# The sample group of an RWKV-7 projection as one step of 160 columns, with its features kept on chip

## The chip, the cores and the metric

The kernel runs as one program on 1 core of a Trainium2 chip. The metric is the device time of one execution in microseconds (us). Of the kernel before there are three timed executions and one that the hardware profiler recorded. PE is TensorE, DVE VectorE, ACT ScalarE, POOL GpSimd and SP SyncE, which here only issues transfers.

## The reference

One step of a decoder trunk for two groups of tokens: a prompt of 2048 tokens, and a sample group of 8 sequences with 4 new tokens each. Both pass through an RMSNorm, a combined projection, RWKV-7 time mixing (8 heads of 64), dilated attention (8 heads of 64), an output projection and a mixture of experts. All is float32. The part that matters here is what the projection hands to the time mixing:

```python
r = r_c + mu[0] * (r_p - r_c)          # c: this token, p: the token before
k = k_c + mu[1] * (k_p - k_c)
v = v_c + mu[2] * (v_p - v_c)
w_log = -softplus(-(w0 + tanh(xw @ w1) @ w2)) - 0.5
decay = exp(-exp(w_log))
a = sigmoid(a0 + (xa @ a1) @ a2)
g = sigmoid(xg @ g1) @ g2
kk = heads(k * k_k)
kk = kk * rsqrt(max(sum(kk * kk, -1), 1e-24))
k_h = heads(k) * (1.0 + (a_h - 1.0) * k_a)
# per token: s = s * w + (s @ -kk) (kk * a) + v k;  y = s @ r
bonus = sum(r_h * k_h * r_k, -1) * v_h
```

## The kernel before

The program is a chain of stages (`projection`, `rwkv_chunks`, `attention`, `output_projection`, the experts). Each stage is a block of five instruction streams, one per engine, written out by hand in the order in which they run and tied by semaphores. The block's end (L54) is a barrier: no engine starts the next stage before all have finished, and SP reaches it only after the stores of the stage have landed.

**The projection.** It takes the 2048 prompt tokens in `NP` = 8 chunks of 256 columns, channels on the partitions. A chunk has four channel groups m = 0..3 of 128 channels. For each group PE multiplies out k, r, v (`channels`), the rates a and the gate g (`rates`), the cumulated log decay (`cumulate`), and two sums over the heads (`norm_sums` for the norm of kk, `bonus_sums`). ACT scales with the token-shift weights (`scale`), applies sigmoid (`rates`), square, exp (`exponents`) and sqrt (`norm_roots`); sigmoid, exp and sqrt each need a table of their own, so each group loads three (`ACT_TABLE_LOAD`). DVE makes five feature rows per token (`mix_k`, `mix_r`, `mix_v`, `bonus_terms`, `recurrence_rows`) and the gate rows (`gate_rows`).

The sample group follows as chunk `n == NP`. It has only `WS` = 40 columns: 8 sequences of 4 tokens with the shifted-in token ahead of each. Its projections are made the other way round, tokens on the partitions: `sample_pair(i)` multiplies two of the six 512-column blocks (k and r, v and query, key and value) with 40 columns as weights, 32 matmuls of 512 columns each. DVE copies the result out (`pair_copy`), and `sample_channels` turns one channel group of k, r or v at a time back to channels on partitions. Then the four groups run through the same code as a prompt chunk, one after the other, 40 columns at a time. `cumulate(NP, m)` waits for `rk_read` of group m - 1, so the groups form one chain. `sample_pair(2)` stands in the middle of group 1.

The recurrence wants the features of two sequences as a tile of 64 token slots each, of which the sample fills 4. POOL therefore clears such rows (`UF` and the projection's weights `W`, four memsets), the groups write into them, and SP stores each group to `ft_s` in device memory (`store_units`): four transfers of 320 KB and one of decays, 4 KB in pieces of 8 bytes. A gate store of 32 KB follows (`store_gates`). ACT may not write the gate of group m before the gate store of group m - 2 has landed (`g_st`). The last stores end the stage.

**The recurrence.** `rwkv_chunks` takes 16 prompt tiles and then 4 sample tiles, n = 16..19, of two sequences each. PE's order is written as iterations: iteration i runs the inverse of tile i, the head (`turn`, products) of tile i + 1 and the tail of tile i - 1. Features sit in a ring of four tiles `F[n % 4]`, each 128 x 2568. SP loads tile n + 4 once the state of tile n is done (`s_ready[1]`). POOL copies identity blocks into `T` for each tile once the tail of tile n - 3 has read them (`hg_done`), and issues three or four stores of zero rows between. The tile's state `s_ready` is DVE's `state`.

## Time and profile before

| | |
|---|---|
| median of 3 executions (lowest, highest) | 3448.79 us (3446.48, 3475.65) |
| the profiled execution, its own time | 3453.1 us |
| its span, mean granted PE clock | 3451.3 us, 0.951 |
| PE, DVE, ACT, POOL busy | 91%, 38%, 29%, 10% |
| projection, from its last prompt matmuls | sample part from 906.2 us |
| recurrence | begins at 982.1 us |

The span is the profiled execution from its first to its last instruction; its own time is 1.8 us more. A PE that is busy 91% of the span still leaves stretches in which it hardly works. The stretch from 906.2 to 982.1 us is one of them: it is the sample group's part of the projection and the wait for its stores. In the rows below, times are counted from the start of the span, "idle before" is what the engine waited and for whom, and a matmul on float32 is recorded as two instructions, a transpose as one.

### The profile page before, as it was taken

How to read it: one execution, taken by the hardware profiler on the slowest of the kernel's cores; microseconds unless marked ns; L12 is line 12 of the kernel's file. 1: busy time of each engine (PE TensorE's matmuls, PEld its weight loads, DVE VectorE, ACT ScalarE, POOL GpSimd, SP SyncE). 2: the span in 40 equal slices, each digit the busy share in tenths (PEclk: the TensorE clock that was granted, in tenths of full speed). 3: DMA queues.
4: the chain of work that ended last, by engine and by line, in shares of the span. 5: the costliest groups of instructions: out<-in, count | busy, mean ns of one | idle time of the engine just before them, and what ended most of it. 6: DMA issues, size and time to landing. Idle time of an engine off the chain costs nothing. (4 is left out here: it accounts for less than half of the span.)

```text
span 3451.3 us, 74888 instructions
## 1 busy us (share of the span) xinstructions
PE 3146.2 (91%) x30921; PEld 2149.7 (62%) x30922; DVE 1318.3 (38%) x3229; ACT 1013.0 (29%) x2151; POOL 338.4 (10%) x351
## 2 busy tenths in 40 slices
PE   6999999999859988988999979996999999999990
PEld 4667666676458888877767765554555555555550
DVE  3455344553224443435655436664111111111117
ACT  3334433344122222225544433331111111111112
POOL 0000000000110000003333000001101001010104
PEclk9999999999979999999999859997999999999995
DMA  6111111111273333326666446423768786677658
GB/s 209 63 71 65 51 46 63 70 55 45 72 180 113 120 137 120 119 98 204 183 182 179 125 162 193 154 80 123 278 242 284 239 283 223 227 277 245 233 193 306
DMA packets 299029, 544.42 MB, mean 158 GB/s; under 512 B 98146, under 2 KB 122466, under 8 KB 292116
## 3 DMA queue, kind: packets, MB, share of 16 engines
q1 hardware_dynamic: 252860, 401.29, 34.6%
q10 hardware_dynamic: 25128, 66.26, 6.1%
q0 software_dynamic: 20784, 73.15, 5.8%
q8 instruction: 197, 3.23, 0.4%
q14 instruction: 60, 0.49, 0.0%
HBM read 400.66 MB, written 139.98 MB: 157 GB/s over the span
## 5 line engine op out<-in xcount | busy, mean ns | idle before, releaser
L307 PE MATMUL proj_main_ps<-proj_xt,proj_w 128*128 128x257 f32 x1536 | 351.1, 381 | 0.0
L307 PEld LDWEIGHTS proj_main_ps<-proj_xt,proj_w 128*128 128x128 f32 x1536 | 290.2, 191 | 41.1
L2544 PE MATMUL moe_y_ps<-moe_w,moe_ht 128*64 128x512 f32 x1312 | 301.2, 601 | 3.1 <-ACT moe_ht L2583 3.1
L2292 PE MATMUL out_proj_ps<-out_w,out_ct 128*128 128x512 f32 x544 | 241.6, 598 | 6.1 <-DMA out_w<-in_w_out_dram 6.1
L337 PE MATMUL proj_main_ps<-proj_w,proj_xt 128*128 128x512 f32 x512 | 225.3, 593 | 0.0
L2594 ACT ACTIVATE moe_sg<-moe_gate 128x256 f32<-128x256 f32 x82 | 31.4, 383 | 535.7 <-PE moe_gate L2528 535.7
L2544 PEld LDWEIGHTS moe_y_ps<-moe_w,moe_ht 128*64 128x64 f32 x1312 | 87.3, 137 | 158.6 <-issue 155.3
L2292 PEld LDWEIGHTS out_proj_ps<-out_w,out_ct 128*128 128x128 f32 x544 | 101.7, 192 | 121.8 <-issue 120.5
L2630 DVE COPY moe_y<-moe_y_ps 128x512 f32<-128x512 f32 x82 | 56.7, 691 | 313.8 <-PE moe_y_ps L2544 313.8
L1190 DVE COPY_PREDICATED rwkv_t<-ahead_rwkv_cons,rwkv_level_ps 128x512 f32<-128x512 uint32 (+1 forms) x168 | 109.1, 660 | 175.7 <-PE rwkv_level_ps L908 175.4
L337 PEld LDWEIGHTS proj_main_ps<-proj_w,proj_xt 128*128 128x128 f32 x512 | 97.2, 190 | 108.4 <-issue 107.0
L1667 DVE CUSTOM_DVE_ANT_0 att_sc<-att_s_ps,ahead_mask 128x256 f32<-128x256 f32 (+1 forms) x384 | 117.2, 361 | 118.4 <-PE att_s_ps L1474 118.4
L908 PE MATMUL rwkv_level_ps<-rwkv_t,rwkv_w 64*64 64x64 f32 x2688 | 153.2, 221 | 2.7 <-issue 2.7
L2528 PE MATMUL moe_up<-moe_w,moe_xt 128*64 128x256 f32 x1344 | 154.3, 382 | 0.0
L2528 PE MATMUL moe_gate<-moe_w,moe_xt 128*64 128x256 f32 x1344 | 152.2, 379 | 0.0
L2579 ACT COPY moe_xt<-moe_xt_ps 128x512 f32<-128x512 f32 x83 | 48.6, 585 | 343.4 <-PE moe_xt_ps L2521 343.4
L2528 PE MATMUL moe_gate<-kept_first_gate,moe_xt 128*64 128x256 f32 x1280 | 147.5, 384 | 1.4 <-ACT moe_xt L2579 1.4
L2528 PE MATMUL moe_up<-kept_first_up,moe_xt 128*64 128x256 f32 x1280 | 146.9, 382 | 0.0
L1576 ACT ACTIVATE att_sc<-att_sc,att_nm 128x256 f32<-128x256 f32 (+1 forms) x384 | 145.6, 451 | 3.9 <-issue 3.1
L1509 PE MATMUL att_o_ps<-att_v,att_pt 128*128 128x65 f32 x768 | 142.0, 301 | 0.0
L2636 DVE TENSOR_TENSOR moe_hd<-moe_sg,moe_gate 128x256 f32<-128x256 f32 x82 | 34.6, 421 | 280.0 <-ACT moe_sg L2594 280.0
L1474 PE MATMUL att_s_ps<-att_kt,ahead_qt 64*128 64x256 f32 (+1 forms) x768 | 139.8, 493 | 0.9 <-DVE att_pt L1675 0.5
(362 smaller groups left out, 5535.3 us busy)
## 6 DMA issues: line engine op xcount, KB each, us to landing
moe_w<-in_expert_w_dram SPq DMA_DIRECT2D x64, 2048.0 KB, 9.6
y_rows<-rwkv_zero POOLq DMA_DIRECT2D x65, 512.0 KB, 4.8
kept_first_gate<-in_expert_w_dram SPq DMA_DIRECT2D x16, 2048.0 KB, 9.6
kept_first_up<-in_expert_w_dram SPq DMA_DIRECT2D x16, 2048.0 KB, 14.9
y_rows<-moe_y ACTq DMA_DIRECT2D x164, 128.0 KB, 6.0
ft_p<-proj_uf SPq DMA_DIRECT2D x32, 642.0 KB, 3.2
rwkv_feat<-ft_p SPq DMA_DIRECT2D x12, 1284.0 KB, 6.9
att_s_k<-in_cache_att_k_dram ACTq DMA_DIRECT2D x14, 1024.0 KB, 6.8
```

The source lines that it names most:

```text
L307: last = mm(out[:, 0:w + 1], W[:, k, kind * C + m * P:kind * C + (m + 1) * P], XT[n % 2][:, k, 0:w + 1], start=(k == 0), stop=(k == KT - 1))
L337: last = mm(out[:], XT[n % 2][:, k, 1 + i // 2 * P:1 + (i // 2 + 1) * P], W[:, k, j * C:(j + 1) * C], start=(k == 0), stop=(k == KT - 1))
L908: last = mm(level_ps[g][part(c), hh * P + DH:(hh + 1) * P], W[g][part(c), hh, :], T[i % 3][part(c), h, DH:P], start=True, stop=True, skip_ ...
L1190: v.copy_predicated(T[i % 3][:, 4 * g:4 * g + 4, k0:P], wide(level(l)[:, k0:P], 4).bitcast(U32), four(level_ps[g][:])[:, :, k0:P]).then_in ...
L1474: last = mm(s_ps[u % 2][e][:, pl * 2 * P + k_from(u):(pl + 1) * 2 * P], QT[rows, q, q_at:q_at + d * (P - 1) + 1:d], KT[rows, q, k_at:k_at ...
L1509: last = mm(out, PT[u % 2][:, hl, 1, :], V[n % NV][:, h, :], start=first(u), stop=True, skip_group_check=True)
L1576: nc.scalar.activation(SC[u % NSC][:, hl, k0:], SC[u % NSC][:, hl, k0:], ACT.Exp, bias=NM[:, n, 4 * half + hl:4 * half + hl + 1], scale=-1 ...
L1667: v.tensor_tensor_reduce(SC[u % NSC][:, hl, k0:], s_ps[u % 2][e][:, pl * 2 * P + k0:(pl + 1) * 2 * P], mask[:, k0:], 1.0, 3e38, ALU.add, A ...
L2292: last = mm(proj_ps[j][:], CT[t % 2][:, k, :], W[:, k, 512 * j:512 * (j + 1)], start=(k == 0), stop=(k == KT - 1))
L2528: last = mm(bank[j * HB:(j + 1) * HB, 0:HF], XT[:, q, r * HB:(r + 1) * HB], W[:, k, j * HF:(j + 1) * HF], start=(k == 0), stop=(k == KT - ...
L2544: last = mm(py[j * HB:(j + 1) * HB, :], HT[:, c, r * HB:(r + 1) * HB], W2[s][:, k, j * 512:(j + 1) * 512], start=(k == 0), stop=(k == FE / ...
L2630: v.tensor_copy(Y[:], py[:]).then_inc(y_ev, 1)
```

## The change

The four channel groups of the sample are no longer run one after the other. PE makes the rates of all four in a row, then pair 1, the four cumulations, the twelve transposes of k, r and v, pair 2, and then one norm sum and one bonus sum over 160 columns, in separate parts of one bank. ACT and DVE treat 160 columns at once where the operand has no constant per channel group, and in four pieces of 40 where it has one. Sigmoid, exp and sqrt are each used once. `NR` is gone: the norms are now made in `KK`, in the prompt's chunks too.

The features go to `sample_feat`, 128 x 5 x 128 on chip, and the decays to `sample_decay`, 128 x 32. They outlive the stage. `ft_s` and its stores are gone, and so are POOL's four memsets in the projection. The gate is stored once, 128 KB. In the recurrence, POOL builds each sample tile (`spread`): one memset of 128 x 2568, two copies of 80 elements per partition and one of 8. PE waits for it (`f_spread`) where it waited for the load.

```diff
                 s = slot(n, m)
                 sp.wait_ge(units, step(n, m) + 1)
                 sp.wait_ge(pc_copied, step(n, m) + 1)
-                if n < NP:
-                    sp.dma_start(ft_p[TT * n:TT * n + TT, :, m, :].rearrange("t p k -> p t k"), UF[:, s]).then_inc(u_st[s], 16)
-                else:
-                    rows = sample_rows_of(m).rearrange("p j (t c) k -> p t j (c k)", c=2)
-                    for t in range(SB // 2):
-                        sp.dma_start(ft_s[t, :, m, 0:5 * P].rearrange("p (j k) -> p j k", j=5), rows[:, t]).then_inc(u_st[s], 16)
-                    sp.dma_start(ft_s[:, :, m, 5 * P:FT].rearrange("t p c -> p t c"), sample_decay_of(m).rearrange("p (t c) -> p t c", c=2)).then_inc(u_st[s], 16)
+                sp.dma_start(ft_p[TT * n:TT * n + TT, :, m, :].rearrange("t p k -> p t k"), UF[:, s]).then_inc(u_st[s], 16)
...
+            sp.dma_start(next_F[0], ft_p[0]).then_inc(feat_ld[0], 16)
+            sp.dma_start(next_consts, next_consts_in).then_inc(cons_ld, 16)
+            sp.dma_start(shift_s_out, XN[SJ - 1:TS:SJ, :]).then_inc(shift_st, 16)
+            for i in range(3):
+                store_kv(NP, i)
+            sp.wait_ge(bonus, 4 * NP + 1)
...
-            g.wait_ge(bonus, 4 * NP)
-            for j in range(2):
-                g.wait_ge(u_st[j], 32 * NP)
-            nc.gpsimd.memset(UF[:], 0.0).then_inc(padded, 1)
-            g.wait_ge(filled, pair_job(1) + 1)
-            for m in range(1, 4):
-                nc.gpsimd.memset(W[:, 0:5, (m - 1) * SB * CH:m * SB * CH], 0.0).then_inc(padded, 1)
...
-            def sample_channels(kind, m):
-                i, part = (0, upper) if kind == 1 else (0, lower) if kind == 0 else (1, upper)
-                out = begin_job(job(NP, (1, 0, 2).index(kind), m))
-                pe.wait_ge(emptied, pair_job(i) + 1)
-                nc.tensor.transpose(out[:, 1:WS + 1], PAIRS[i][part, m * P:(m + 1) * P], ident[part, part]).then_inc(filled, 1)
...
+            def sample_turn_kr():
+                pe.wait_ge(emptied, pair_job(0) + 1)
+                for m in range(4):
+                    sample_turn(0, upper, x_ps, m * WS, m)
+                    last = sample_turn(0, lower, lz_ps[1], m * WS, m)
+                last.then_inc(s_turned, 1)
+
+            def sample_turn_v():
+                pe.wait_ge(emptied, pair_job(1) + 1)
+                pe.wait_ge(ag_read, 4 * NP + 1)
+                for m in range(4):
+                    last = sample_turn(1, upper, ag_ps, m * WS, m)
+                last.then_inc(s_v_turned, 1)
+
...
+            def sample_cumulate():
+                pe.wait_ge(z_ready, NP + 1)
+                pe.wait_ge(rk_read, 4 * NP)
+                for m in range(4):
+                    last = mm(own(c_ps, m), Z[0:WS, 0, m * P:(m + 1) * P], cum_s[0:WS, :], start=True, stop=True, skip_group_check=True)
+                last.then_inc(cum_done, 1)
+
+            def sample_norm_sums():
+                pe.wait_ge(sq_ready, 4 * NP + 1)
+                pe.wait_ge(exps, 4 * NP + 1)
+                mm(c_ps[:, SW:2 * SW], same_head, SQ[:, 0:SW], start=True, stop=True, skip_group_check=True).then_inc(kk_done, 1)
+
+            def sample_bonus_sums():
+                pe.wait_ge(rk_ready, 4 * NP + 1)
+                pe.wait_ge(root, 4 * NP + 1)
+                mm(c_ps[:, 2 * SW:3 * SW], same_head, RK[:, 0:SW], start=True, stop=True, skip_group_check=True).then_inc(rk_done, 1)
 
...
             sample_pair(1)
-            for m in range(4):
-                sample_channels(1, m)
-                if m >= 1:
-                    rates(NP, m)
-                    bonus_sums(NP, m - 1)
-                sample_channels(0, m)
-                cumulate(NP, m)
-                sample_channels(2, m)
-                norm_sums(NP, m)
-                if m == 1:
-                    sample_pair(2)
-            bonus_sums(NP, 3)
+            sample_cumulate()
+            sample_turn_kr()
+            sample_turn_v()
+            sample_pair(2)
+            sample_norm_sums()
+            sample_bonus_sums()
 
...
             def norm_roots(n, m):
                 u = step(n, m)
                 a.wait_ge(kk_done, u + 1)
                 if u >= 1:
-                    a.wait_ge(unit, u)
-                nc.scalar.sqrt(NR[:, 0:width(n)], c_ps[:, 0:width(n)]).then_inc(root, 1)
+                    a.wait_ge(units, u)
+                nc.scalar.sqrt(KK[:, 0:width(n)], c_ps[:, 0:width(n)]).then_inc(root, 1)
+
+            def sample_rate_acts():
+                a.wait_ge(s_rated, 1)
+                a.wait_ge(units, 4 * NP)
+                for m in range(4):
+                    last = act(own(A, m), own(ag_ps, m), ACT.Sigmoid, bias=col(A0, m))
...
+            def sample_exponents():
+                a.wait_ge(cum_done, 4 * NP + 1)
+                a.wait_ge(units, 4 * NP)
+                act(EXS[:, 1:SW + 1], c_ps[:, 0:SW], ACT.Exp, scale=-DECAY)
+                act(EX2[:, 0:SW], c_ps[:, 0:SW], ACT.Exp, scale=DECAY).then_inc(exps, 1)
+                a.wait_ge(exps, 4 * NP + 1)
+                nc.scalar.copy(sample_decay, EXS[:, 1:SW + 1].rearrange("p (b j) -> p b j", j=SQ1)[:, :, SQ1 - 1]).then_inc(pc_copied, 1)
+
+            def sample_roots():
+                a.wait_ge(kk_done, 4 * NP + 1)
+                a.wait_ge(units, 4 * NP)
+                nc.scalar.sqrt(KK[:, 0:SW], c_ps[:, SW:2 * SW]).then_inc(root, 1)
 
             square(0)
...
+            sample_rate_acts()
+            sample_exponents()
+            sample_scale_kr()
+            sample_squares()
+            sample_scale_v()
+            sample_roots()
             for i in range(1, 3):
...
+            def sample_recurrence_rows():
+                u = 4 * NP
+                tok = lambda x: tokens(x[:, 0:SW])
+                v.wait_ge(exps, u + 1)
+                v.tensor_tensor(sample_unit(1), tok(R), tok(EXS[:, 1:]), ALU.mult)
+                v.tensor_tensor(sample_unit(3), tok(KH), tok(EX2), ALU.mult)
+                v.wait_ge(root, u + 1)
+                v.tensor_scalar(KK[:, 0:SW], KK[:, 0:SW], 1e-12, None, ALU.max).then_inc(bound, 1)
+                v.wait_ge(bound, u + 1)
+                v.reciprocal(KK[:, 0:SW], KK[:, 0:SW]).then_inc(inverse, 1)
+                v.wait_ge(inverse, u + 1)
+                for m in range(4):
+                    last = stt(own(KK, m), own(K, m), col(K_K, m), own(KK, m), ALU.mult, ALU.mult)
+                last.then_inc(unit, 1)
+                v.wait_ge(unit, u + 1)
+                stt(sample_unit(0), tok(KK), -1.0, tok(EXS), ALU.mult, ALU.mult).then_inc(a_done, 1)
+                v.wait_ge(a_done, u + 1)
+                v.tensor_tensor(KK[:, 0:SW], KK[:, 0:SW], A[:, 0:SW], ALU.mult).then_inc(kka, 1)
+                v.wait_ge(kka, u + 1)
+                v.tensor_tensor(sample_unit(2), tok(KK), tok(EX2), ALU.mult).then_inc(units, 1)
+
+            def sample_gate_rows():
+                v.wait_ge(rk_done, 4 * NP + 1)
+                v.wait_ge(s_v_mixed, 1)
+                v.tensor_tensor(tokens(RK[:, 0:SW]), sample_unit(4), tokens(c_ps[:, 2 * SW:3 * SW]), ALU.mult).then_inc(rk_read, 1)
+                v.wait_ge(rk_read, 4 * NP + 1)
+                for m in range(4):
+                    last = stt(by_seq(sample_gates[:, m, 1, :]), tokens(own(RK, m)), col(LN_B, m), tokens(own(GG[0], m)), ALU.add, ALU.mult)
+                last.then_inc(bonus, 1)
 
...
         def _(sp):
             def load(n):
-                sp.dma_start(F[n % 4][:], ft_p[n] if n < NP else ft_s[n - NP]).then_inc(f_ld[n % 4], 16)
+                sp.dma_start(F[n % 4][:], ft_p[n]).then_inc(f_ld[n % 4], 16)
...
-                if n + 4 < NT:
+                if n + 4 < NP:
...
+            def spread(n):
+                g.wait_ge(s_ready[1], n - 3)
+                nc.gpsimd.memset(F[n % 4][:], 0.0).then_inc(f_cleared, 1)
+                g.wait_ge(f_cleared, n - NP + 1)
+                rows = F[n % 4][:, :, 0:5 * P].rearrange("p m (j c k) -> p m j c k", j=5, c=2)
+                for c in range(2):
+                    nc.gpsimd.tensor_copy(rows[:, :, :, c, 0:given_feat.shape[4]], given_feat[:, :, :, 2 * (n - NP) + c, :])
+                nc.gpsimd.tensor_copy(F[n % 4][:, :, 5 * P:FT], given_decay[:, :, 2 * (n - NP):2 * (n - NP) + 2]).then_inc(f_spread, 1)
+
...
+                if n >= NP:
+                    spread(n)
                 if n >= 3:
...
                 if half == 0:
-                    pe.wait_ge(f_ld[n % 4], 16 * (n // 4 + 1))
+                    if n < NP:
+                        pe.wait_ge(f_ld[n % 4], 16 * (n // 4 + 1))
+                    else:
+                        pe.wait_ge(f_spread, n - NP + 1)
```

PE, projection, after the low-rank products of the sample. L320 is `sample_pair`, L347 the decay's projection, L354 and L355 the rates, L314 the transposes, L365 `cumulate`, L371 and L376 the two head sums. Before:

```order
L320 MATMUL proj_main_ps<-proj_w,proj_xt 40x512 x16
L314 MATMUL proj_main_ps<-proj_consts,proj_x 128x40 x2
L365 MATMUL proj_c_ps<-proj_consts,proj_z 128x40
L314 MATMUL proj_main_ps<-proj_consts,proj_x 128x40
L371 MATMUL proj_c_ps<-proj_sq,proj_consts 128x40
L314 MATMUL proj_main_ps<-proj_consts,proj_x 128x40
L354 MATMUL proj_ag_ps<-proj_lta,proj_a 128x40
L355 MATMUL proj_ag_ps<-proj_ltg,proj_g 128x40
L376 MATMUL proj_c_ps<-proj_rk,proj_consts 128x40
L314 MATMUL proj_main_ps<-proj_consts,proj_x 128x40
...
L371 MATMUL proj_c_ps<-proj_sq,proj_consts 128x40
L320 MATMUL proj_main_ps<-proj_w,proj_xt 40x512 x16
```

Now (L335 `sample_pair`, L310 and L311 the rates, L318 cumulations, L291 the transposes, L324 and L329 the head sums):

```order
L362 MATMUL proj_lz_ps<-proj_w2x,proj_ltw 40x512
L310 MATMUL proj_ag_ps<-proj_lta,proj_a 128x40
L311 MATMUL proj_ag_ps<-proj_ltg,proj_g 128x40
...
L335 MATMUL proj_main_ps<-proj_w,proj_xt 40x512 x16
L318 MATMUL proj_c_ps<-proj_consts,proj_z 128x40 x4
L291 MATMUL proj_x_ps<-proj_consts,proj_x 128x40
L291 MATMUL proj_lz_ps<-proj_consts,proj_x 128x40
...
L291 MATMUL proj_ag_ps<-proj_consts,proj_x 128x40 x4
L335 MATMUL proj_main_ps<-proj_w,proj_xt 40x512 x16
L324 MATMUL proj_c_ps<-proj_sq,proj_consts 128x160
L329 MATMUL proj_c_ps<-proj_rk,proj_consts 128x160
```

The third pair moved from the middle of group 1 to a place behind every transpose and ahead of both head sums, and the head sums of four groups became one each.

ACT, projection, one group of the sample (group 1) before; L497 to L504 are the rates, L481 `scale`, L511 the squares, L521 to L530 the exponents, L537 the roots:

```order
L497 ACT_TABLE_LOAD
L497 ACTIVATE proj_a<-proj_ag_ps,proj_par 128x40
...
L504 ACTIVATE proj_kh<-proj_a,proj_less,proj_par 128x40
L481 ACTIVATE proj_ev<-proj_main_ps,proj_par 128x40
L511 ACTIVATE proj_sq<-proj_k,proj_par 128x40
L521 ACT_TABLE_LOAD
L521 ACTIVATE proj_exs<-proj_c_ps 128x40
L522 ACTIVATE proj_ex<-proj_c_ps 128x40
L530 COPY proj_w<-proj_exs 128x8
L481 ACTIVATE proj_ev<-proj_main_ps,proj_par 128x40
L537 ACT_TABLE_LOAD
L537 ACTIVATE proj_nr<-proj_c_ps 128x40
```

Now, from the rates of all groups to the end of the stage's arithmetic:

```order
L542 ACTIVATE proj_a<-proj_ag_ps,proj_par 128x40 x4
L547 COPY proj_gg<-proj_ag_ps 128x160
L549 ACTIVATE proj_gb<-proj_ag_ps,proj_par 128x32 x4
L553 ACTIVATE proj_kh<-proj_a,proj_less,proj_par 128x40 x4
L581 ACT_TABLE_LOAD
L581 ACTIVATE proj_ex<-proj_c_ps 128x160
L582 ACTIVATE proj_ex<-proj_c_ps 128x160
L561 ACTIVATE proj_ev<-proj_x_ps,proj_par 128x40 x4
...
L575 ACTIVATE proj_sq<-proj_k,proj_par 128x40 x4
L589 ACT_TABLE_LOAD
L589 ACTIVATE proj_kk<-proj_c_ps 128x160
```

Three table loads per group became two for all groups, since the first sigmoid finds its table loaded. The exponents moved ahead of the scaling of k and r.

SP, the end of the projection, before (L188 the sample's query, key and value rows, L166 and L167 `store_units`, L175 the gate; one group of four is shown) and now:

```order
L188 DMA qkv_s<-proj_x 8x512 x8
L166 DMA ft_s<-proj_w 128x5x128 x4
L167 DMA ft_s<-proj_w 128x4x2
L175 DMA gt_s<-proj_gb 128x2x32
L166 DMA ft_s<-proj_w 128x5x128 x4
L167 DMA ft_s<-proj_w 128x4x2
L175 DMA gt_s<-proj_gb 128x2x32
L54 UNCONDITIONAL_BRANCH
```

```order
L224 DMA ahead_feat<-ft_p 128x2568
L225 DMA ahead_rwkv_cons<-in_const_rwkv_chunks_dram 128x1280
L226 DMA out_dram<-proj_xn 8x1024
L180 DMA qkv_s<-proj_x 8x512 x12
L230 DMA gt_s<-proj_gb 128x256
L54 UNCONDITIONAL_BRANCH
```

Twenty transfers to `ft_s` and three gate stores are gone, and nothing stands behind the one gate store that is left.

## Rows read from the trace of the kernel before

**Rows 1.** Windows of the stage's end: engines busy (instructions), clock granted, DMA share, GB/s

```profile
945.10:967.20 22.10, 6.08 (x28) 4.96 (x27) 8.59 (x41) 12.63 (x30) 0.00 (x0) 0.61 0.98 126
967.20:982.10 14.90, 0.00 (x0) 0.00 (x0) 0.00 (x0) 0.00 (x0) 0.00 (x0) 0.50 0.91 102
```

**Rows 2.** Timeline where the two orders part: start us, us, engine, line, operation

```profile
915.28 0.41 PE L354 MATMUL proj_ag_ps<-proj_lta,proj_a 64*128 64x40 f32 x2
...
915.96 7.07 PE L320 MATMUL proj_main_ps<-proj_w,proj_xt 128*40 128x512 f32 x32
...
922.96 0.26 PE L314 MATMUL proj_main_ps<-proj_consts,proj_x 40*128 40x40 f32 x2
...
923.04 0.39 PE L365 MATMUL proj_c_ps<-proj_consts,proj_z 40*128 40x40 f32 x2
```

**Rows 3.** Groups of instructions, 906.2 to 967.2 us: count, busy, mean ns, idle before

```profile
L521 ACT ACT_TABLE_LOAD x4 | 5.1, 1283 | 0.1
L537 ACT ACT_TABLE_LOAD x4 | 5.1, 1283 | 0.1
L497 ACT ACT_TABLE_LOAD x3 | 3.8, 1283 | 6.2 <-DVE proj_w L662 3.4 <-DVE proj_uf L662 2.8
```

**Rows 4.** Timeline, sample group 0 and the start of group 1

```profile
923.10 6.58 POOL L270 MEMSET proj_w<- 128x2560 f32 x3 [51.05 <-PE proj_main_ps L320]
...
926.46 0.62 PE L371 MATMUL proj_c_ps<-proj_sq,proj_consts 128*128 128x40 f32 x2 [2.32 <-ACT proj_ex L522]
...
928.30 1.42 DVE L651 TENSOR_SCALAR proj_nr<-proj_nr 128x40 f32<-128x40 f32 x1 [1.17 <-ACT proj_nr L537]
...
931.22 1.28 ACT L497 ACT_TABLE_LOAD   x1 [2.77 <-DVE proj_uf L662]
...
932.51 0.29 ACT L497 ACTIVATE proj_a<-proj_ag_ps,proj_par 128x40 f32<-128x40 f32 x1
```

**Rows 5.** Timeline, pair 2 in the middle of group 1

```profile
936.09 8.93 PE L320 MATMUL proj_main_ps<-proj_w,proj_xt 128*40 128x512 f32 x32
```

**Rows 6.** Timeline, the same chain at 40 columns (group 2) and at 256 (prompt)

```profile
861.97 0.38 ACT L537 ACTIVATE proj_nr<-proj_c_ps 128x256 f32<-128x256 f32 x1
...
866.15 0.43 DVE L662 TENSOR_TENSOR proj_uf<-proj_kk,proj_ex 128x256 f32<-128x256 f32 x1
...
866.72 0.60 DVE L611 SCALAR_TENSOR_TENSOR proj_mixed<-proj_diff,proj_mu,proj_xt 128x40 f32<-128x40 f32 x3
...
953.37 0.20 ACT L537 ACTIVATE proj_nr<-proj_c_ps 128x40 f32<-128x40 f32 x1
...
955.01 0.19 DVE L662 TENSOR_TENSOR proj_w<-proj_kk,proj_ex 128x32 f32<-128x32 f32 x1
```

**Rows 7.** Timeline, end of the stage and start of the next

```profile
952.46 5.15 SPq L188 DMA_DIRECT2D qkv_s<-proj_x  x8
...
966.89 0.25 DVE L671 SCALAR_TENSOR_TENSOR proj_gb<-proj_rk,proj_par,proj_gg 128x32 f32<-128x32 f32 x1
...
972.88 1.55 SPq L175 DMA_DIRECT2D gt_s<-proj_gb  x1
...
982.10 1.29 SPq L823 DMA_DIRECT2D rwkv_feat<-ft_p  x3
```

**Rows 8.** Waits of SP's queue, 900 to 1500 us: total, times, longest

```profile
SPq L245 <- DMA gt_s<-proj_gb: 7.0, 1, 7.0
```

**Rows 9.** Transfers, whole span: KB each, median us from issue to landing

```profile
qt_p<-proj_q SPq DMA_DIRECT2D x32, 128.0 KB, 1.7
```

**Rows 10.** Timeline of the recurrence: sample tile 19 fetched, and shortly before its turn

```profile
1497.43 0.32 SPq L823 DMA_DIRECT2D rwkv_feat<-ft_s  x1
...
1500.85 0.91 DVE L1190 COPY_PREDICATED rwkv_t<-ahead_rwkv_cons,rwkv_level_ps 128x256 f32<-128x256 uint32 x2 [3.44 <-PE rwkv_level_ps L908]
...
1520.61 1.11 PE L1027 MATMUL rwkv_head_ps<-ahead_rwkv_cons,rwkv_nat 128*128 128x128 f32 x4 [3.15 <-DMA rwkv_nat<-in_state_rwkv_dram]
```

**Rows 11.** Timeline, POOL's clearing of 2568 elements in the projection

```profile
869.82 2.24 POOL L267 MEMSET proj_uf<- 128x2568 f32 x1 [173.35 <-DMA ft_p<-proj_uf]
```

More of the change, by code:

```diff
@@ L209, in _ @@
             load_next(3)
-            for n in range(NP + 1):
+            for n in range(NP):
                 for m in range(4):
@@ new lines, in sample_squares @@
+            def sample_squares():
+                a.wait_ge(s_mixed, 1)
+                a.wait_ge(kk_done, 4 * NP)
+                for m in range(4):
+                    last = act(own(SQ, m), own(K, m), ACT.Square, scale=col(K_K, m))
+                last.then_inc(sq_ready, 1)
+            def sample_exponents():
[5 more added lines that the diff above has]
+                nc.scalar.copy(sample_decay, EXS[:, 1:SW + 1].rearrange("p (b j) -> p b j", j=SQ1)[:, :, SQ1 - 1]).then_inc(pc_copied, 1)
```

250 lines of the change are left out of this document (141 added, 109 removed).

## The prediction

> **What bounds the kernel now.** I read the windows of the projection's end first, then the order of instructions there, then the waits, and last the recurrence. Over the whole run PE is busy 91%, so only stretches where PE does little can be shortened. From 945.1 to 967.2 us PE is busy 6.08 of 22.1 us, ACT 12.63 and DVE 8.59: no engine is full, so a chain of waits sets the pace. From 967.2 to 982.1 us no engine does anything while the DMA engines are 0.91 busy [rows 1]: these are the stores. What is to be seen is that the sample's part of the stage consists of a chain at 40 columns, where fixed costs count and widths do not, and of a tail of transfers.
>
> Within a group, each table load takes 1.28 us and falls on the chain, because it is started only after the wait for the product that needs it [rows 3, 4]. There are 4 for exp, 4 for sqrt and 3 for sigmoid from 923 us on. PE's clock is granted at a mean of 0.61 of full speed from 945.1 us and at 0.50 from 967.2 (0.50 is 1.2 GHz, 1.00 is 2.4 GHz), and pair 2 takes 8.93 us where pair 1 takes 7.07 [rows 1, 2, 5].
>
> **The change, part by part.** Both orders agree up to 915.28 us, where the rates begin [rows 2]. I lay the new chain from there.
>
> 1. Rates of four groups: the two matmuls of one group take 915.28 to 915.96, 0.68 us. Four take 2.72, to 918.00. Before, one group stood ahead of pair 1.
> 2. Pair 1, by the starts 915.96 and 922.96: 7.00 us, to 925.00 [rows 2].
> 3. Four cumulations of 0.39 us each at most: 1.56, to 926.56. Twelve transposes, two in 0.26 us: 1.56, to 928.12 [rows 2]. The transposes of v wait for DVE's copy of pair 1, 512 columns wide and begun at 925.1, and for ACT's rate work, which has 7 us during pair 1 for 13 instructions; both are done by about 926.
> 4. Pair 2 directly behind: 7.00, to 935.12. That takes the full clock. PE has no gap over a few tenths between 915 and 935 now, while the clock fell before only after the gap of 2.32 us ahead of 926.46 [rows 4].
> 5. Behind pair 2, ACT and DVE must not be late. After 926.56: table 1.28, two exponentials of 0.38 (the width of 256 is an upper bound), a copy 0.20, eight scalings of 0.29, eight DVE mixes of 0.20 (three take 0.60), four squares of 0.29 [rows 4, 6]. Without any overlap that is 926.56 + 1.28 + 0.96 + 2.32 + 1.60 + 1.16 = 933.9 us. So the norm sum starts when pair 2 ends, and all this costs nothing; without pair 2 as cover it would be up to 5.8 us.
> 6. Norm sum over 160 columns: 0.60 us, the 0.62 of the narrow one at low clock being near [rows 4]. To 935.7.
> 7. Table for sqrt, 1.28 us, to 937.0.
> 8. From the start of sqrt to the last feature row: 953.37 to 955.20, 1.83 us, at 40 columns, and 861.97 to 866.58, 4.61 us, at 256 [rows 6]. In a straight line, 160 columns give 1.83 + 2.78 x 120/216 = 3.37. The product with k_k is now four pieces, three more starts of 0.18 us from three in 0.60: +0.53. To 940.9.
> 9. Gate rows: one product of about 0.3 and four pieces, 0.78. To 942.0, against 967.14 before [rows 7]. The chain gains **25.1 us**.
>
> The tail: before, the last arithmetic ends at 967.14 and the next stage starts at 982.10, 14.96 us. The last gate store is issued at 972.88, held up by five stores ahead of it, and SP waits 7.0 us more for it [rows 7, 8]. Now the same wait has one store of 128 KB, 1 KB per partition, behind it nothing. The query stores are of just that size and shape and land in a median of 1.7 us [rows 9]. With 0.8 us to see the last result, issue and pass the barrier, 2.5 us. This end could also be as slow as now: 7.0 + 1.55 + 0.6 = 9.2 us [rows 7, 8]. I take 2.5, because the 7.0 stands behind 1.3 MB of feature stores in pieces of 512 and of 8 bytes that no longer exist. The 16 small stores of queries, keys and values that are left by then are issued by SP and ACT side by side, 8 each. SP took 5.15 us for eight of them before [rows 7], so from 935.8 on to 941, before the gate. The tail gains **12.4 us**.
>
> The rest of the edits. Sqrt into `KK` in the prompt's chunks waits for `units` instead of `unit`; ACT has already waited for `units` of the same step ahead of the exponents, so nothing. The carry copies on POOL have no memset behind them, nothing. In the recurrence POOL adds per tile a memset of 2.24 us [rows 11] and three copies of at most 80 elements, 1.2 us together if each is 0.4. The tile's predecessor is free at 1497.4 us, when SP now issues the load, and PE turns tile 19 only after 1520.61 [rows 10]. 3.5 us fit into 23 us; the identity copy of the same tile has the time of one iteration too. Cost nothing, and if that cover were gone, 3.5 us for each of four tiles.
>
> Sum: 25.1 + 12.4 = **37.5 us**, from 3453.1 of the profiled execution to 3415.6. Its own time lies 4.3 us above the median of the three, so against that median **3411.3 us**, 1.1% less.
>
> A table load has no wait behind it in the trace: it starts at 931.22, takes 1.28 and sigmoid starts at 932.51 [rows 4]. The Trainium skill (ScalarE: Activation LUTs, What ACT_TABLE_LOAD costs) puts a drain of 1.38 us beside the load of 1.283, 2.66 us in all. By it, step 7 would be 1.4 us longer and the result 3412.7 us; the load's own figure agrees with the trace, the drain does not.
>
> **The rivals.**
>
> A. The gate store lands late. It starts while 16 small stores are in flight, 8 rows of 2 KB each from few partitions. For it: every gate store of the sample waited long before. Against it: those had the feature stores ahead. At the 9.2 us above: 30.8 us gained, 3418 us. Chance 0.15.
>
> B. The clock falls before pair 2. The transposes and cumulations are 40 columns wide and small work. Then pair 2 takes 8.93 instead of 7.00, and cumulations and transposes twice as long in part, +1.5, and the head sum a little more: 34 us gained, 3415 us. Against it: pair 1 ran at full speed behind narrow matmuls too. Chance 0.12.
>
> C. POOL's memset holds up DVE. One memset of POOL ran from 923.10 to 929.68, and DVE's maximum on `proj_nr`, one input and output on chip, took 1.42 us from 928.30 and ended at 929.72, with it; products with two inputs went on beside it [rows 4]. In the recurrence a memset of 2.24 us starts when a state is done. DVE's next work there comes 3.44 us after its last [rows 10], so 1.2 us at most would stick out behind memset and copies, and no DVE instruction there is of the kind that was held. If each were held for the full 2.24 us: 9 us back, 3420 us. Chance 0.08.
>
> The Trainium skill (SBUF — State Buffer, Who interferes with whom) has it as a lock on a port pair that the two share: whoever comes second waits for the whole instruction, if DVE uses both ports or has two inputs on chip while POOL reads. That rule speaks against moving clearing work beside DVE; the row of 1.42 us agrees with it.
>
> D. Slower than before. `spread` becomes what PE waits for. PE waits in order at `turn`, so everything behind stands. It decides only above the cover of 23 us a tile; to be 1% slower than before, four tiles would have to lose 37.5 + 34.5 = 72 us, 18 each, so one `spread` would have to last 41 us. That would happen if the strided copies of 80 elements took some 19 us each, and would give about 3483 us. Nothing in the trace is near: POOL clears 2568 elements in 2.24 us [rows 11]. Chance 0.03.
>
> **How the numbers follow.** The forecast has 0.62, A 0.15, B 0.12, C 0.08, D 0.03. The predicted time is that of the forecast. The range goes down to 3404, where steps 3, 6 and 8 are over by 3 us and executions scatter by 3 or 4 us, and up to 3425, above the cases A to C and two of them partly together; outside are D, the larger combinations and a disturbed set of executions. What a measurement can tell here from no change is about 1%, 34.5 us, and 3414.3 us is the bound. The forecast lies 3 us beyond it, so I give it 0.78 to pass; B 0.4, A and C 0.15: 0.48 + 0.05 + 0.04 = 0.57 faster. Slower 0.03, the rest 0.40 the same.
>
> **What would show it.** In the profile of the changed kernel: the next stage starts near 944.5 us; pair 2 takes 7.1 us and the norm sum stands right behind it (if it is idle before, step 5 is wrong); two table loads behind the rates; the last gate row near 942; one gate store landing in about 2 us (9 means A); no wait of PE for POOL in the recurrence, whose length from its start stays within 2 us (C or D otherwise). The prediction would be wrong if the recurrence or a later stage became longer by what the projection gives.

## The result, and the profile after

The changed kernel takes 3396.05 us (median of 4 executions, 3392.17 to 3402.42), the kernel before 3457.14 in the same comparison (4 executions): ratio 0.984, 95% interval 0.980 to 0.989. Two more comparisons gave 0.988 (0.984 to 0.993) and 0.986 (0.982 to 0.990), over 1% faster in each. The forecast was 3411.3 us with a range from 3404: the direction is right, the time fell below the range. Three later executions of 5036 to 8071 us, far slower than all others, are left out of every figure below.

The profiled execution has a span of 3399.8 us against 3451.3, so 51.5 us are to be placed. I take the same marks in both traces: the copy of pair 0 by DVE, the first copy of `rwkv_t` (recurrence), the copy of `rwkv_sv` (its end), the first product of `out_ct` (attention's end).

| us | before | changed | gained |
|---|---|---|---|
| up to pair 0's copy | 914.5 | 913.8 | 0.8 |
| from there to the recurrence | 67.6 | 28.2 | 39.4 |
| recurrence | 592.3 | 593.2 | -0.9 |
| attention | 482.4 | 470.5 | 11.9 |
| all that follows | 1394.5 | 1394.1 | 0.4 |

The projection gives 39.4 us, where the prediction had 37.5. Another 11.9 come from attention, whose code the change doesn't touch.

First the windows of the changed sample part, which answer to [rows 1]:

```profile
core 0: us, PE busy (x) PEld busy (x) DVE busy (x) ACT busy (x) POOL busy (x), PEclk, DMA share, GB/s
914.50:925.80 11.30, 11.30 (x71) 5.75 (x70) 0.69 (x1) 5.28 (x17) 0.00 (x0) 1.00 0.01 1
925.80:932.80 7.00, 7.00 (x34) 1.89 (x33) 3.25 (x17) 4.81 (x19) 0.00 (x0) 1.00 0.03 11
932.80:938.10 5.30, 1.02 (x6) 0.57 (x4) 5.00 (x17) 0.30 (x1) 0.00 (x0) 0.75 0.08 28
938.10:942.00 3.90, 0.00 (x0) 0.00 (x0) 0.02 (x1) 0.00 (x0) 0.00 (x1) 0.50 0.19 63
```

PE is busy without a gap, at the full clock, until pair 2 is done; only 5.3 us are left in which DVE alone is the chain, and the tail is 3.9 us instead of 15. Now the order of instructions of the changed kernel in time, the chain's links only:

```profile
914.52 0.41 PE L310 MATMUL proj_ag_ps<-proj_lta,proj_a 64*128 64x40 f32 x2
...
917.27 7.07 PE L335 MATMUL proj_main_ps<-proj_w,proj_xt 128*40 128x512 f32 x32
...
920.38 1.28 ACT L581 ACT_TABLE_LOAD   x1
924.26 0.86 PE L318 MATMUL proj_c_ps<-proj_consts,proj_z 40*128 40x40 f32 x6
...
925.38 0.31 ACT L581 ACTIVATE proj_ex<-proj_c_ps 128x160 f32<-128x160 f32 x1 [3.72 <-PE proj_c_ps L318]
...
925.78 7.07 PE L335 MATMUL proj_main_ps<-proj_w,proj_xt 128*40 128x512 f32 x32
...
930.03 0.82 ACT L568 ACTIVATE proj_ev<-proj_ag_ps,proj_par 128x40 f32<-128x40 f32 x4
930.87 1.28 ACT L589 ACT_TABLE_LOAD   x1
...
932.77 0.54 PE L324 MATMUL proj_c_ps<-proj_sq,proj_consts 128*128 128x160 f32 x2
...
933.35 0.30 ACT L589 ACTIVATE proj_kk<-proj_c_ps 128x160 f32<-128x160 f32 x1 [1.20 <-PE proj_c_ps L324]
...
933.62 6.52 ACTq L635 DMA_DIRECT2D out_dram<-proj_x  x8
...
933.90 0.23 DVE L776 TENSOR_SCALAR proj_kk<-proj_kk 128x160 f32<-128x160 f32 x1
934.17 1.15 DVE L778 RECIPROCAL proj_kk<-proj_kk 128x160 f32<-128x160 f32 x1
...
937.38 0.74 DVE L796 SCALAR_TENSOR_TENSOR proj_gb<-proj_rk,proj_par,proj_gg 128x32 f32<-128x32 f32 x4
939.06 0.68 SPq L230 DMA_DIRECT2D gt_s<-proj_gb  x1
941.99 1.28 SPq L935 DMA_DIRECT2D rwkv_feat<-ft_p  x3
```

Both table loads stand ahead of the instruction that needs them, and in ScalarE's idle time: each ends before PE's product does. The chain's last row ends at 938.12 (967.14 before), the recurrence starts at 941.99 (982.10 before, [rows 7]).

Last, the recurrence's new work, POOL's instructions in order of time for tile 16 (answers to the memset of [rows 11]):

```profile
1382.70 2.24 POOL L983 MEMSET ahead_feat<- 128x2568 f32 x1 [20.47 <-DVE rwkv_s L1344]
1385.00 0.45 POOL L987 COPY ahead_feat<-ahead_sample_feat 128x80 f32<-128x80 f32 x2
1385.39 0.20 POOL L988 COPY ahead_feat<-ahead_sample_decay 128x8 f32<-128x8 f32 x1
1388.97 1.04 POOL L997 COPY rwkv_t<-ahead_rwkv_cons 128x1024 f32<-128x1024 f32 x1 [3.39 <-PE rwkv_tail_ps L1096]
```

A spread lasts 2.9 us, and POOL then idles 3.39 us for PE. No row has PE waiting for POOL.

### The profile page after: what moved, and what is told of

Read it like the earlier page. It is cut to its first block and busy times, and to the rows that moved or that the text cites. A ratio compares the mean times of both kernels' runs of the same rounds, so it can differ in the third digit from the quotient of the medians.

```text
span 3399.8 us, 74730 instructions
## 1 busy us (share of the span) xinstructions
PE 3123.1 (92%) x30909; PEld 2127.4 (63%) x30910; DVE 1311.9 (39%) x3202; ACT 999.8 (29%) x2127; POOL 342.5 (10%) x362
## 5 line engine op out<-in xcount | busy, mean ns | idle before, releaser
L1031 PEld LDWEIGHTS rwkv_level_ps<-rwkv_t,rwkv_w 64*64 64x64 f32 x2688 | 134.9, 137 | 8.1 <-issue 8.1
```

Of the source, the lines that this page charges most:

```text
L1031: last = mm(level_ps[g][part(c), hh * P + DH:(hh + 1) * P], W[g][part(c), hh, :], T[i % 3][part(c), h, DH:P], start=True, stop=True, skip_ ...
```

## The experiments

Theory 1: the change is worth what the projection's chain and tail give, and the 12 us of attention are chance. Theory 2: the change also shortens attention. Beside these, single terms of the sum are measured.

**before_again** and **after_again**: the two kernels unchanged.

> The kernel before, once more. The change took 51.5 us off the profiled span, 40.1 of it by the start of the recurrence and 12 in the attention stage (last state copy of the recurrence to the first head product of the output projection: 482.3 us before, 470.5 changed), which the change does not touch. Theory 1 (chance): TensorE's clock falls to 0.50 for some tens of us while TensorE is fully busy in attention, in a place and for a length that differs from execution to execution; then attention here is anywhere between 465 and 485 us, and the ratio of this kernel to itself is 1.000 within about 0.005. Theory 2 (caused): attention is again within 3 us of 482.

> The changed kernel, once more. Theory 1: the attention stage may well be 475 us or more in this profile, and over many executions the change is worth what the projection gives, 39 to 40 us (ratio 0.9885). Theory 2: attention is within 3 us of 470.5 again and the ratio is about 0.985, 51 to 54 us. Both expect the recurrence to start at 942 us.

Measured: the kernel before 3440.33 us (12 executions) against its own 3439.89 (29 more), ratio 1.000 (0.997 to 1.004); the changed kernel 3398.26 (6), ratio 0.988 (0.984 to 0.993). In their profiled executions the sample part takes 66.1 and 28.2 us, attention 466.0 and 462.7. So the gain of attention is 3.3 us here and was 11.9: it isn't a property of the change alone. The windows show what is. Kernel before, then the same stretch (391 us into attention) of before_again:

```profile
1954.50:1961.60 7.10, 7.10 (x17) 2.36 (x15) 0.00 (x0) 0.00 (x0) 0.00 (x0) 1.00 0.21 52
1961.60:1965.00 3.40, 3.40 (x25) 3.02 (x26) 2.92 (x11) 0.74 (x3) 0.00 (x0) 0.84 0.02 5
1965.00:2010.00 45.00, 45.00 (x239) 41.01 (x238) 16.29 (x108) 22.68 (x72) 0.00 (x0) 0.50 0.27 73
```

```profile
1963.60:2008.60 45.00, 45.00 (x329) 37.86 (x327) 21.97 (x146) 29.22 (x91) 0.00 (x0) 1.00 0.35 91
```

PE is busy all 45 us in both, but at 0.50 it gets through 239 matmuls and at 1.00 through 329 (a rough comparison, since the second stretch begins some 7 us earlier in the program, with 3.6 us of the long products named below in it). It fell behind 7.1 us in which PE had only the sample's products of values, with every other engine at 0.00:

```profile
1954.53 6.17 PE L1529 MATMUL att_t_ps<-att_s_v,att_s_lm 128*96 128x512 f32 x14
1960.63 1.09 PE L1530 MATMUL att_t_ps<-att_s_vn,att_s_pn 4*96 4x512 f32 x2
```

The same products stand there in every execution, and in 11 of 14 profiled ones the clock stays at this place. In the changed kernel's trace it fell earlier, 189 and 237 us into attention, also directly behind such products (at 1721.4 and 1770.5 us), and for some 10 us each. Over the 14 profiled executions of all kernels here I added up the time at half clock in windows of 1 us in which PE was busy 90% or more: attention took 459 to 463 us where it was 4 to 16 us, 466 to 475 where it was 27 to 51, and 480 to 482 where it was 74 to 79.

**compact_groups**: the features on chip and `spread`, but still four groups one after the other.

```diff
-                    for t in range(SB // 2):
-                        sp.dma_start(ft_s[t, :, m, 0:5 * P]..., rows[:, t]).then_inc(u_st[s], 16)
+        unit_of = ... sample_feat[:, j, m * TS:(m + 1) * TS].rearrange("p (b j) -> p b j", j=SJ)   # n == NP, group m
```

> Compact storage alone: the sample's four groups run one after the other as before, but write into the compact buffer; no memsets and no feature stores in the projection, four small gate stores, POOL spreads the tiles in the recurrence. If storage and chain are two separate gains: the maximum held up by the memset gets its 1.2 us back, the wait of 3.6 us for a gate store goes, the tail shrinks from 15.0 to about 4, so the recurrence starts at 982.1 - 16 = 966 us, and the one step of 160 columns is worth the other 24. If the rival holds that the one step does nearly all (the feature stores were hidden by it anyway), the start is 975 or later. Attention: theory 1 any value, theory 2 about 470.

Measured: 3421.31 us (10), ratio 0.993 (0.990 to 0.996). The sample part takes 52.8 us (51.5 expected). So, taken in this order, the compact storage gives about 14 us (66.1 or 67.6 less 52.8) and the one step of 160 columns 24.6 (52.8 less 28.2). Its eleven table loads (four for exp, four for sqrt, three for sigmoid) are still on the chain; a sigmoid's, and the queue's first gate stores, in time order:

```profile
932.63 1.28 ACT L479 ACT_TABLE_LOAD   x1 [1.53 <-DVE ahead_sample_feat L641]
...
933.19 17.22 SPq L165 DMA_DIRECT2D gt_s<-proj_gb  x2
```

**stores_kept**: the changed kernel with the 20 feature stores put back behind the last feature row; what they write isn't read.

```diff
+            sp.wait_ge(units, 4 * NP + 1)
+            for m in range(4):
+                for t in range(SB // 2):
+                    sp.dma_start(ft_s[t, :, m, 0:5 * P].rearrange("p (j k) -> p j k", j=5), rows[:, t]).then_inc(u_st[0], 16)
+                sp.dma_start(ft_s[:, :, m, 5 * P:FT]...).then_inc(u_st[0], 16)
```

> The changed kernel with the 20 feature stores of the kernel before put back behind the last feature row, from a buffer that nobody reads (the recurrence still takes the compact features). Issuing them takes SP some 15 us (0.55 to 0.7 each, more for the four of 8-byte pieces) and the gate store behind them lands some 7 us later as before: the recurrence starts at 938 + 15 + 1 + 7 + 1 = 962 us instead of 942. If the stores were cheap (all hidden in the DMA queues), 946. Attention: theory 1 any value; theory 2, if it is the address of the tensors in device memory that counts, 482 again, since the scratch tensor is back.

Measured: 3433.39 us (10), ratio 0.999 (0.996 to 1.002); sample part 64.4 us, 36 more than in the changed kernel, where 20 were expected. SP's queue in order of time:

```profile
941.38 3.45 SPq L234 DMA_DIRECT2D ft_s<-proj_uf  x4
944.87 1.09 SPq L235 DMA_DIRECT2D ft_s<-proj_uf  x1
946.00 3.71 SPq L234 DMA_DIRECT2D ft_s<-proj_uf  x4
949.75 1.09 SPq L235 DMA_DIRECT2D ft_s<-proj_uf  x1
950.89 6.40 SPq L234 DMA_DIRECT2D ft_s<-proj_uf  x4
957.33 2.90 SPq L235 DMA_DIRECT2D ft_s<-proj_uf  x1
960.27 7.29 SPq L234 DMA_DIRECT2D ft_s<-proj_uf  x4
967.61 2.38 SPq L235 DMA_DIRECT2D ft_s<-proj_uf  x1
970.04 1.77 SPq L237 DMA_DIRECT2D gt_s<-proj_gb  x1
978.89 1.29 SPq L942 DMA_DIRECT2D rwkv_feat<-ft_p  x3
```

The first eight stores of 320 KB cost SP 0.9 us each to issue, the last eight 1.6 and 1.8 (6.40 and 7.29 for four). The same bytes therefore cost more when they come in a row than between groups, and the gate store behind them again needs 7.1 us from its issue to the next stage, against 2.25 without them. (In stores_more below, the same kernel, the last eight cost 1.9 and 2.1 us each and the gate store needs 8.9.) That is the 7.0 of [rows 8], made and unmade by the stores ahead: rival A is refuted, and the choice of a short landing stands.

The run shows one thing more: the one step alone, with the stores left in, is worth next to nothing. The sample part takes 64.4 us here and 68.8 in stores_more, against 66.1 to 70.1 in three profiles of the kernel before, since all 20 stores now come in a row behind the last feature row. The 14 and 24.6 us above hold where the compact storage comes first; with the one step first the shares are about 1 us for the step and 38 for the storage.

**load_waits**: the order of two waits ahead of sqrt.

```diff
             def sample_roots():
+                a.wait_ge(units, 4 * NP)
                 a.wait_ge(kk_done, 4 * NP + 1)
-                a.wait_ge(units, 4 * NP)
```

> The two waits ahead of sqrt on ScalarE stand in the other order, so that its table load waits for the norm sum on TensorE instead of running while pair 2 is computed. Theory 1 (the order of the waits decides, and a load costs 1.28 us as in its row): the load starts when the norm sum ends, sqrt starts 1.28 us after that instead of at once, and the last gate row comes 1.3 us later, at about 32.6 + 1.3 = 33.9 us after the copy of pair 0 begins (32.6 in the changed kernel, 938.12 less 905.49 for the last product before). The recurrence starts only 0.4 to 1.3 us later, since SyncE is at its stores until 0.9 us after that last row now. Rival (load and drain both count, 2.66 us): sqrt starts 2.7 us after the sum, and the recurrence starts 1.8 to 2.7 us later.

Measured (one execution, 3390.44 us, so only the trace is read):

```profile
935.22 0.54 PE L324 MATMUL proj_c_ps<-proj_sq,proj_consts 128*128 128x160 f32 x2
...
935.84 1.28 ACT L589 ACT_TABLE_LOAD   x1 [2.55 <-PE proj_c_ps L324]
...
937.14 0.30 ACT L589 ACTIVATE proj_kk<-proj_c_ps 128x160 f32<-128x160 f32 x1
```

The load now waits for PE, and the last gate row comes 25.5 us after pair 0's copy instead of 24.3: 1.2 us, theory 1. A load and a drain (2.66) would have been 2.7. The recurrence still starts 28.2 us after that copy. The extra 1.2 us vanish in slack: SP had been busy with its twelve small stores until 0.9 us behind the last row, and ScalarE's eight stores end only 1.85 us ahead of the next stage in both.

**spread_long**: four memsets per spread instead of one.

```diff
-                nc.gpsimd.memset(F[n % 4][:], 0.0).then_inc(f_cleared, 1)
-                g.wait_ge(f_cleared, n - NP + 1)
+                for k in range(4):
+                    nc.gpsimd.memset(F[n % 4][:], 0.0).then_inc(f_cleared, 1)
+                    g.wait_ge(f_cleared, 4 * (n - NP) + k + 1)
```

> Each of the four tiles of the sample is cleared four times over by POOL, so that a spread takes 9.0 us of clearing and 1.1 of copies instead of 3.3. Theory 1 (spread is under the cover of 23 us, and the recurrence's length varies by itself between 583 and 593 us): no wait of TensorE for POOL, the last four intervals between the copies of y sum to 72 to 75 us as in the kernels before and changed, time 3398 us, within 10. Rival C (POOL's clearing holds up VectorE for its whole length): 6.7 us more for each of four tiles, 27 us in all, 3425 us. Rival D (TensorE waits for the spread): up to 7 us a tile as well, with a wait of TensorE for POOL in the trace.

Measured: 3395.22 us (9), ratio 0.987 (0.984 to 0.991), as the changed kernel.

```profile
1382.07 9.13 POOL L984 MEMSET ahead_feat<- 128x2568 f32 x4 [20.22 <-DVE rwkv_s L1345]
1391.26 0.45 POOL L988 COPY ahead_feat<-ahead_sample_feat 128x80 f32<-128x80 f32 x2
```

Recurrence 587.4 us, inside the 583 to 598 of all kernels here; no wait of PE for POOL. Rivals C and D are refuted for this place: a spread over three times as long is still covered.

**idle_added** and **idle_short**: the changed kernel with 20 or 8 memsets of a dead tile on POOL behind pair 2's copy.

```diff
+            g.wait_ge(emptied, pair_job(2) + 1)
+            for k in range(20):
+                nc.gpsimd.memset(UF[:]..., 0.0).then_inc(set_up, 1)
```

> The changed kernel with 20 clearings of a dead tile on POOL behind the copy of pair 2, while every other engine has nothing to do: the recurrence starts about 38 us later, near 980, as in the kernel before, and nothing else is changed. It asks whether time saved in the projection is kept whole by what follows. Theory 1 (the recurrence and attention don't depend on when they start; what differs there between two executions is chance): 3398 + 38 = 3436 us, within 6, and lengths of recurrence and attention inside what the other executions have (583 to 594 and 460 to 483). Rival (idle TensorE time is paid back by less time at half clock in attention later, or the other way, the saved time brought the 12 us more in attention): the whole differs from 3398 by under 28 us (or by over 48).

> The changed kernel with 8 clearings of a dead tile on POOL behind the copy of pair 2, so that the recurrence starts 12 us later and nothing else is changed. Without executions of the upper group: 3395 + 12 = 3407 us, within 5. Theory 1: the share of the upper group as in the changed kernel. Rival (the instant at which attention reaches those products decides, and a shift of 12 us moves it): another share than the changed kernel, and than the one with 38 us of idle time, which had none in 12.

Measured: sample part 67.9 and 40.3 us; time 3427.65 (12), ratio 0.996 (0.993 to 0.999), and 3410.2 (5), ratio 0.989 (0.985 to 0.994). The means lie 29.4 us above the changed kernel's for 39.7 us of delay (standard error 3.4) and 12.5 for 12.1 (5.6). The short one fits whole; of the long one only three quarters arrive, between the bounds set for the theories (32 and 28) and nearer the rival. By its ratio it is 13 us under the kernel before, which starts the recurrence at the same instant. Its profiled attention is 459.2 us without such a fall of the clock; idle_short's is 480.1 with 68 us in a row at half clock.

One thing more stood in these two traces. DVE's maximum over 160 columns in idle_added:

```profile
935.67 9.13 POOL L255 MEMSET proj_uf<- 128x2568 f32 x4 [239.64 <-DVE proj_x L750]
...
935.93 2.08 DVE L782 TENSOR_SCALAR proj_kk<-proj_kk 128x160 f32<-128x160 f32 x1
938.04 1.15 DVE L784 RECIPROCAL proj_kk<-proj_kk 128x160 f32<-128x160 f32 x1
939.23 0.77 DVE L787 SCALAR_TENSOR_TENSOR proj_kk<-proj_k,proj_par,proj_kk 128x40 f32<-128x40 f32 x4
```

It takes 2.08 us instead of 0.23, and is over at 938.01, about when the first of the memsets (2.28 us each) is; the reciprocal and the products beside the later memsets take what they take alone. That is rival C's mechanism at its full length, and as narrow as [rows 4] had it: of these instructions only this one kind. It agrees with the lock that the Trainium skill (SBUF — State Buffer, Who interferes with whom) describes, for the maximum; that reciprocal isn't held is what these rows show.

**after_more**, **before_more**, **stores_more**: three kernels again, to count executions.

> The changed kernel once more. Attention has shown two lengths so far: 459 to 471 us, and 482 us where TensorE's clock is granted at 0.5 for its last 67 us, behind the sample's products of values 384 us in. Theory 1 (which of the two comes is chance and the change has no part in it): about as many executions in the upper group as of the kernel before, a fourth to a third. Theory 2 (the change makes the upper group rarer): at most a tenth or so, and a mean gain above the 39 us that the projection gives.

> The kernel before once more, 12 executions or so beside those of the comparison. Of 63 so far 20 lay in the upper group, from 3448 us on. Both theories: the same share again. If the share is far lower here, it belongs to the chip or the hour and not to the kernel, and theory 2 has nothing to stand on.

> The changed kernel with the 20 stores of features put back behind the last row (their result is not read). Theory 1: the same share of the upper group as in the changed kernel. Theory 2, in the form that the stores or the late start make it frequent: a third again (4 of 10 before), while the changed kernel has a tenth.

Measured: changed kernel 3393.48 us (6), ratio 0.986 (0.982 to 0.990); ratio 1.000 (0.997 to 1.003) for the kernel before; with the stores 3433.51 (12), ratio 0.996 (0.993 to 0.999). The mean granted clock of each execution sorts them: of 96 executions of the kernel before in the three comparisons, 30 have 0.953 or less and a mean of 3458.5 us, 66 have more and a mean of 3436.1. Of the changed kernel's 16, one has 0.953 or less (3429.93 us), and two more stand apart (3409.62 and 3414.42, at 0.957 and 0.955; its mean clock is higher anyway, as it has 39 us less of waiting, much of it at 0.50). From 1 or 3 of 16 nothing follows against 30 of 96. But all kernels with the features on chip together can be held against the kernel before, by their means, less what their sample part gives (67.9 us before, the mean of three profiles):

| | executions | mean us | under 3443.1 | of it sample part | left, with standard error |
|---|---|---|---|---|---|
| changed kernel | 16 | 3399.1 | 44.0 | 39.2 | 4.8 (3.1) |
| compact_groups | 10 | 3421.6 | 21.5 | 15.1 | 6.4 (1.6) |
| stores (both runs) | 22 | 3435.3 | 7.8 | 1.3 | 6.5 (2.7) |
| idle_added | 12 | 3428.5 | 14.6 | 0.0 | 14.6 (2.2) |

All four have something left, 5 to 15 us. The standard errors cover the times alone; the sample part of one kernel differs by up to 4.4 us between profiles (64.4 and 68.8), and all four rows share one mean of the kernel before. So only idle_added's rest is clear of every error, and the changed kernel's 4.8 is not. Theory 2 has something for it, at a size that stays open. The start of the stages isn't the reason (idle_added starts as late as before), nor are the stores.

Nor does the rest look the same everywhere. compact_groups has none of its ten executions at 0.953 or less, and that is its whole rest: 3421.6 and 15.1 are 3436.7, the mean of the kernel before's 66 executions above 0.953 being 3436.1. idle_added's eleven executions above 0.953 have a mean of 3427.4, well under those 66. What the four kernels share is the recurrence's supply, `spread` in place of four loads of 1.3 MB. Their recurrence, with that of the other kernels that have it, lasts 583 to 596 us in eleven profiles (mean 589) and 590 to 598 in the three of the kernel before (mean 593): 4 us, of the size of the rest, but with a standard error of 3. Whether the rest lies there or in the clock of attention is not shown.

In after_more's trace pair 1 took 8.59 us instead of 7.07, at a clock of 0.81: rival B's mechanism, one pair earlier, for 1.5 us.

**pairs_swapped**: a version that the slack suggests. Keys and values for the cache are pair 1, v and q pair 2; the norm sum stands inside pair 2; ScalarE copies pair 2 and issues 4 stores instead of 8.

```diff
-                    for part, j in zip((upper, lower), ((1, 0), (2, 3), (4, 5))[i]):
+                    if i == 2 and k == KT - 3:
+                        sample_norm_sums()
+                    for part, j in zip((upper, lower), ((1, 0), (4, 5), (2, 3))[i]):
```

> A variant of the changed kernel: keys and values for the cache are the second pair, v and q the third; the norm sum stands inside the third pair behind its fifth of eight steps; ScalarE copies the third pair and stores q, SyncE stores the rest; VectorE mixes v last. Theory 1 (the end of the projection now hangs on pair 2, then on 3.1 us of roots and reciprocal, then on the stores queued ahead of the gate store): the last gate row comes 1 us earlier than 938.1 and SyncE issues the gate store right behind it, so that the stage from the copy of pair 0 to the recurrence takes 26.3 us instead of 28.2; in the whole time that is 2 us, below what three rounds can tell from nothing: 3396 us, within 6. Rival (the stage is bound by the number of small stores, 20 on two queues, whatever their order): 28 us or more.

Measured: the sample part takes 26.0 us (26.3 expected, 28 by the rival), the time 3400.08 (4), ratio 0.987 (0.980 to 0.994): 2.2 us better in the stage, not to be told from the changed kernel in the whole.

```profile
929.85 0.54 PE L326 MATMUL proj_c_ps<-proj_sq,proj_consts 128*128 128x160 f32 x2 [0.16 <-ACT proj_sq L578]
...
931.11 0.30 ACT L592 ACTIVATE proj_kk<-proj_c_ps 128x160 f32<-128x160 f32 x1
...
936.29 0.74 DVE L799 SCALAR_TENSOR_TENSOR proj_gb<-proj_rk,proj_par,proj_gg 128x32 f32<-128x32 f32 x4
937.05 0.34 SPq L232 DMA_DIRECT2D gt_s<-proj_gb  x1
939.49 1.28 SPq L937 DMA_DIRECT2D rwkv_feat<-ft_p  x3
```

## Why the prediction was right about the stage and wrong about the time

| step | predicted us | measured us |
|---|---|---|
| 1 rates | 2.72 | 2.75 |
| 2 pair 1 | 7.00 | 6.99 |
| 3 cumulations, transposes | 3.12 | 1.52 |
| 4 pair 2 | 7.00 | 6.99 |
| 5 ACT, DVE beside it | 0 | 0 |
| 6 norm sum | 0.60 | 0.58 |
| 7 table for sqrt | 1.28 | 0 |
| 8 roots to feature row | 3.90 | 3.71 |
| 9 gate rows | 1.1 | 1.06 |
| tail | 2.5 | 3.87 |

- **The chain** gained 28.3 us instead of 25.1. Step 3 was twice too long: I priced each of the 16 small matmuls by a row in which two come in a group, and in a row of 16 they follow each other every 0.1 us. Step 7 had a wrong reading of [rows 3, 4] under it, that a table load starts only after the wait for the product that needs it. No load of the sample's groups did. In [rows 3] the loads for exp and sqrt stand 0.1 us behind ScalarE's last instruction; the first sqrt's starts while the product of 926.46 (0.62 us, [rows 4]) is still running:

```profile
926.77 1.28 ACT L537 ACT_TABLE_LOAD   x1
```

  They were on the chain because ScalarE came to them late, not because they waited. The sigmoid's load in [rows 4] waits for `units`, the line directly ahead of the sigmoid; its product's wait is the line before that. In the changed kernel the line directly ahead of exp and of sqrt is again `units`, long satisfied, so both loads ran ahead of the product. load_waits put the product's wait there, and the load waited: 1.2 us back.
- **The drain** of the Trainium skill (ScalarE: Activation LUTs, What ACT_TABLE_LOAD costs), which would have added 1.4 us: in load_waits the load takes 1.28 us and sqrt starts 0.02 us behind it. This trace shows the load's figure and no drain.
- **The tail** is 3.87 us instead of 2.5. The gate store's landing was as taken (2.25 us from the end of its issue to the next stage), but SP reached it 0.9 us late, behind its twelve small stores, which were put down as done by then. That the projection's 39.4 us lie so near to 37.5 is in part luck: 3.2 us too little in the chain and 1.4 too much in the tail.
- **Covers.** Step 5, the free sqrt into `KK`, the free carry copies and the free spread held; spread_long shows room for a spread three times as long.
- **Rivals.** A, C in the recurrence and D didn't occur; B did in one other execution, small.
- **The step that failed** is in how the numbers follow: "executions scatter by 3 or 4 us", and the time before as the median of three. The 96 later executions of the kernel before lie between 3421 and 3470 us, with a standard deviation of 12.3 us and a median of 3441.0. So the base of 3448.79 was 8 us high, and the range's lower end had no room for that: from 3441.0 the same sum gives 3403.5. Of the 15.2 us between forecast and time the base is 7.8, the projection's 39.4 instead of 37.5 is 1.9, and 5.5 are left (3448.79 - 3396.05 - 7.8 - 39.4), of the size of the rest in the table above. By the means the change is worth 44.0 us, with a standard error of 3.1: 39 of them are shown to be the projection's, and the other 5 are some 1.5 standard errors and have no known cause. The last line of the prediction had said that a later stage could take away what the projection gives; that it could add was not in the cases.

## What to carry to other kernels

Where a stage at its end keeps no engine busy, count the links of its chain and the stores ahead of its last store, not the busy time: merging four narrow steps and dropping 20 stores gave 39 us together, with nearly the same arithmetic, while the merge with the stores left in gave about 1. Put the next long matmul behind the small work, so that table loads and narrow steps lie beside it, and check which wait stands directly ahead of an instruction that loads a table. Before a forecast of 1% is set against three executions, look in the trace for a stretch at half clock with PE fully busy: the one here was worth some 20 us (attention 480 to 482 us with it, 459 to 475 without), over half a per cent, and came and went between executions of one kernel.

## What was not expected of the hardware

- The granted clock of PE fell to 0.50 with PE busy all the time, and stayed there for 68 to 72 us until attention's matmuls were over or nearly so, in 3 of the 14 profiled executions; before it lay 7 us of sample products with every other engine idle. In the other 11 the clock is at 1.00 behind these products.
- An issue of a 320 KB store costs SP 0.9 us for the first eight in a row, and 1.6 to 2.1 us for the next eight (stores_kept, stores_more).
- A memset of POOL stretched DVE's one-input maximum from 0.23 to 2.08 us; the reciprocal and the products beside the next memsets kept their usual times.
- The recurrence's length differs by up to 12 us between executions of one kernel (583.4 in stores_kept, 595.5 in stores_more), and one iteration by 8.6 us. The clock has a part in it: the iteration of 38.3 us (stores_more, from 1135.16) ran at a mean of 0.87, the one of 29.7 us (stores_kept, from 1131.98) at 1.00. The rest stays unexplained.
